# Two transformer blocks on one core: slots of the first and last round that span all four experts, tokens copied by halves

## The reference

```python
g_sel = argmax(x @ w_rg + b_rg)                        # one of 4 groups
e_sel = (x @ w_re + b_re)[group g_sel]                 # 8 logits
top_p, top_i = top_k(softmax(e_sel), 2)                # two experts
y = sum over the two: weight * (silu(x @ w_gate[e]) * (x @ w_up[e])) @ w_down[e]
```

## Time and profile before

| what | value |
|---|---|
| median of 3 runs | 1939.9 us (1939.42 to 1945.66) |
| the profiled execution | 1944.58 us, span 1942.9 us |
| mean granted PE clock | 0.918 of full |
| PE busy | 1547.8 us, 80% of the span |
| DVE, ACT, POOL busy | 424.6, 248.7, 86.5 us |
| HBM read | 708.17 MB, 365 GB/s over the span |

### The profile page before, as it was taken

The page is one execution under the profiler, slowest core; times in us unless marked ns, Lnnn a source line. Parts: engine busy times, 40 slices in busy tenths (PEclk is TensorE's granted clock), DMA queues, the critical chain, the costliest instruction groups (busy, mean ns, idle before and its releaser), DMA issues.

```text
span 1942.9 us, 23298 instructions
## 1 busy us (share of the span) xinstructions
PE 1547.8 (80%) x10236; PEld 749.9 (39%) x10236; DVE 424.6 (22%) x944; ACT 248.7 (13%) x531; POOL 86.5 (4%) x142
## 2 busy tenths in 40 slices
PE   7898777899888788999977677776798777576676
PEld 4654434764454344444522122221354222122222
DVE  3341111226331112464500000000043000000001
ACT  0310000126221011155100000000011000000000
POOL 1100000101100000112100000000000000000000
PEclk9999989999999899999998888888899888878888
DMA  7559999869869999299499999999986999999996
GB/s 283 220 217 404 423 423 423 298 225 388 314 270 410 413 421 419 94 363 399 191 403 424 423 424 423 424 424 424 423 328 269 424 424 424 424 423 424 424 423 268
DMA packets 122894, 711.11 MB, mean 366 GB/s; under 512 B 8376, under 2 KB 13480, under 8 KB 49056
## 3 DMA queue, kind: packets, MB, share of 16 engines
q1 hardware_dynamic: 116368, 697.14, 87.7%
q0 software_dynamic: 4320, 9.78, 1.4%
q10 hardware_dynamic: 2096, 2.57, 0.5%
HBM read 708.17 MB, written 1.05 MB: 365 GB/s over the span
## 4 chain that ended last, share of the span: by engine, by line
PE 46%; DMA 42%; DVE 5%; SPq 3%; ACT 2%; issue 2%; POOL 0%; DVEq 0%; ACTq 0%; PEldq 0%; POOLq 0%
DMA ring<-in_moe_w 22%; DMA ring<-in_moe_w_down 9%; PE pa L757 7%; PE pb L740 6%; DMA work<-in_moe_w 5%; PE pa L775 4%; PE acc L819 3%; PE pb L725 3%; DMA ring<-in_moe_w_up 3%; PE acc L1314 3%; PE acc L1319 3%; SPq L681 2%; PE acc L1059 2%; PE acc L1233 2%; DMA mod<-in_moe_w 2%
## 5 line engine op out<-in xcount | busy, mean ns | idle before, releaser
L740 PE MATMUL pb<-ring,XT 128*32 128x512 f32 x1488 | 274.7, 702 | 91.2 <-DMA ring<-in_moe_w 82.4
L757 PE MATMUL pa<-ring,work 128*32 128x512 f32 x1056 | 220.2, 754 | 75.7 <-DMA ring<-in_moe_w 43.9
L740 PEld LDWEIGHTS pb<-ring,XT 128*32 128x32 f32 x1488 | 64.5, 125 | 255.5 <-issue 124.7
L819 PE MATMUL acc<-XT,work 128*128 128x512 f32 x256 | 118.4, 605 | 35.2 <-DVE XT L875 22.4
L865 DVE TENSOR_TENSOR work<-work,pb 128x256 f32<-128x256 f32 (+1 forms) x32 | 17.8, 555 | 574.3 <-PE pb L740 433.7
L775 PE MATMUL pa<-work,HM 128*128 128x128 f32 x1024 | 128.4, 287 | 18.2 <-issue 18.2
L775 PEld LDWEIGHTS pa<-work,HM 128*128 128x128 f32 x1024 | 126.8, 203 | 33.0 <-issue 33.0
L740 PE MATMUL pb<-work,XT 128*32 128x512 f32 x480 | 112.0, 688 | 26.5 <-DMA work<-in_moe_w 26.5
L757 PEld LDWEIGHTS pa<-ring,work 128*32 128x32 f32 x1056 | 48.5, 132 | 200.8 <-issue 88.9
L725 PE MATMUL pb<-ring,XT 128*32 128x256 f32 x1728 | 111.7, 385 | 11.8 <-DMA ring<-in_moe_w_up 7.3
L757 PE MATMUL pa<-work 128*32 128x512 f32 x384 | 86.3, 747 | 22.0 <-DMA work<-in_moe_w 13.2
(11 more groups left out here) (404 smaller groups left out, 1741.5 us busy)
## 6 DMA issues: line engine op xcount, KB each, us to landing
ring<-in_moe_w SPq DMA_DIRECT2D x135, 2048.0 KB
work<-in_moe_w SPq DMA_DIRECT2D x46, 2048.0 KB
ring<-in_moe_w_up SPq DMA_DIRECT2D x28, 2048.0 KB
ring<-in_moe_w_gate SPq DMA_DIRECT2D x26, 2048.0 KB
ring<-in_moe_w_down SPq DMA_DIRECT2D x24, 2048.0 KB
ring<-in_w_mod SPq DMA_DIRECT2D x48, 1024.0 KB
mod<-in_moe_w SPq DMA_DIRECT2D x11, 2048.0 KB
work<-in_moe_w_down SPq DMA_DIRECT2D x8, 2048.0 KB
```

The costliest lines, as they stand in the source:

```text
L740: last = nc.tensor.matmul(hbank[m][j * CAP:(j + 1) * CAP, :], m_xg[:, k, j * CAP:(j + 1) * CAP], slot_of(s0 + j // 2)[:, at:at + fn], star ...
L757: last = nc.tensor.matmul(pa[j * CAP:(j + 1) * CAP, h, :], m_ht[:, c, j * CAP:(j + 1) * CAP], slot_of(i)[:, at:at + 512], start=(c == 0), ...
L819: last = nc.tensor.matmul(acc[:, tt, h * 512:(h + 1) * 512], m_pwt[:, tt * P:(tt + 1) * P], m_yg[:, 4 * h:4 * h + 4, :], start=False, stop ...
```

## The change

- `across` (new): in round 0 the first two slots, and in round 7 all down slots, span all four experts. A slot of the gate matrix then holds half of its rows (wide: half of the first half's) for four experts; a down slot holds one chunk of 128 hidden values for four experts. Each slot is given back by itself. In the last round the constant products stand between the chunks, 8 at a time, in place of 10 between the slots of a pair.
- The gather counts each half. ACT copies the first bank after the first half. The gate products wait for that copy alone; the wait for DVE's copies (`second_banks`) stands before chunk 4 (narrow) or before the up matrix (wide). Rounds 6 and 7 of stage 2 keep the wait in front, and so do rounds of a further pass.
- `rows_tensor` stands behind the first matrix (narrow: the gate; wide: its first half), but for those two rounds.
- Routing: 2 constant products in place of 8 before tile 1's transposes; new ones before the logits, 2 for tile 1 and, in the wide stages, 4 for tile 0.

```diff
+        def across(fn, g, i):
+            down = moe_slots(fn) - fn // P
+            if g == 0 and i < 2:
+                return 0, 0, i
+            if g == ROUNDS - 1 and i >= down:
+                return 2, (i - down) // 2, (i - down) % 2
+            return None
@@ router_tensor
-                    warm_tensor(pe, pb[:, 0, :], 8)
+                    warm_tensor(pe, pb[:, 0, :], 2)
...
+                if t or ph.fn == FN2:
+                    warm_tensor(pe, (pb[:, 0, :], pa[:, 1, :])[t], (4, 2)[t])
                 pe.wait_ge(xt_ready, 4 * ph.xt + 2 * (t + 1))
@@ whole_sync
+                slot_free(sp, q)
+                if across(ph.fn, g, i):
+                    w, half, u = across(ph.fn, g, i)
+                    src = names[w][g * SIDE:(g + 1) * SIDE].rearrange("j (h p u r) f -> h u p j (r f)", h=ph.fn // FN1, p=P, u=2)[half, u]
+                    sp.dma_start(slot(q).rearrange("p (j f) -> p j f", j=SIDE), src).then_inc(full[at[q].slot], FILL)
+                    continue
@@ new, called by whole_up_tensor for the first matrix of round 0
+        def across_up_tensor(fn, rows, s0, bank, wait_full, free, slot_of, n, at_half=None):
+            for k in range(n):
+                if at_half and k == n // 2:
+                    at_half()
+                if k % rows == 0:
+                    wait_full(s0 + k // rows)
+                held = slot_of(s0 + k // rows).rearrange("p (j r f) -> p j r f", j=SIDE, r=rows)
+                for j in range(SIDE):
+                    last = nc.tensor.matmul(bank[j * CAP:(j + 1) * CAP, :], m_xg[:, k, j * CAP:(j + 1) * CAP],
+                                            held[:, j, k % rows, :], start=(k == 0), stop=(k == KC - 1))
+                if k % rows == rows - 1:
+                    last.then_inc(*free)
@@ whole_up_tensor, narrow
+                    if across(fn, g, 2 * m):
+                        across_up_tensor(fn, KC // 2, 0, hbank[m], wait_full, free, slot_of, KC, second_banks)
+                        rows_tensor(pe, ph, g)
+                        continue
                     for k in range(KC):
+                        if m == 0 and k == KC // 2:
+                            second_banks()
...
-                    if m == 0:
+                    if m == 0 and context_round(ph, g):
                         context_tensor(pe, ph, g)
+                    elif m == 0:
+                        rows_tensor(pe, ph, g)
@@ whole_up_tensor, wide
+                    if s0 == 2:
+                        second_banks()
+                        rows_tensor(pe, ph, g)
+                    if across(fn, g, s0):
+                        across_up_tensor(fn, KC // 4, s0, hbank[m], wait_full, free, slot_of, KC // 2)
+                        continue
@@ whole_down_tensor
+            if g == ROUNDS - 1:
+                for c in range(n_down):
+                    if c:
+                        warm_tensor(pe, pb[:, 1, :], 8)
+                    wait_full(n_up + c)
+                    held = slot_of(n_up + c).rearrange("p (j f) -> p j f", j=SIDE)
+                    for h in range(2):
+                        for j in range(SIDE):
+                            last = nc.tensor.matmul(pa[j * CAP:(j + 1) * CAP, h, :], m_ht[:, c, j * CAP:(j + 1) * CAP],
+                                                    held[:, j, h * 512:(h + 1) * 512], start=(c == 0), stop=(c == n_down - 1))
+                    last.then_inc(*free)
+                return
...
-                            if g == ROUNDS - 1 and j:
-                                warm_tensor(pe, pb[:, 1, :], 10)
@@ round_tensor
-            last.then_inc(r["gathered"], 1)
+                if k % (KC // 2) == KC // 2 - 1:
+                    last.then_inc(r["gathered"], 1)
...
-            pe.wait_ge(r["pwt_copied"], t + 1 + START)
             pe.wait_ge(r["ht_copied"], t + START)
-            pe.wait_ge(r["xg_copied"], 2 * (t + 1) + START)
+            pe.wait_ge(r["xg_first"], t + 1 + START)
+            def second_banks():
+                pe.wait_ge(r["xg_copied"], t + 1 + START)
+                pe.wait_ge(r["pwt_copied"], t + 1 + START)
             if whole:
-                rows_tensor(pe, ph, g)
-                whole_up_tensor(pe, ph, g, wait_full, free, slot_of, hbank)
+                if context_round(ph, g):
+                    second_banks()
+                    rows_tensor(pe, ph, g)
+                whole_up_tensor(pe, ph, g, wait_full, free, slot_of, hbank, second_banks)
+            else:
+                second_banks()
@@ round_scalar
-            act.wait_ge(r["gathered"], t + 1 + START)
-            nc.scalar.copy(m_xg[:, 0:4, :], pa[:, 0, :].rearrange("p (k c) -> p k c", c=P)).then_inc(r["xg_copied"], 1)
+            act.wait_ge(r["gathered"], 2 * t + 1 + START)
+            nc.scalar.copy(m_xg[:, 0:4, :], pa[:, 0, :].rearrange("p (k c) -> p k c", c=P)).then_inc(r["xg_first"], 1)
```

More of the change, by code:

```diff
@@ L525, in build_model @@
         R = [{n: sem(f"{n}{k}") for n in (
-            "p_ready", "pw_ready", "rank_next", "gathered", "xg_copied", "pwt_ps", "pwt_copied", "silu_done", "hh_ready", "ht_ps", "ht_copied", "y_copied", "added")} for k in ("", "_x")]
+            "p_ready", "pw_ready", "rank_next", "gathered", "xg_first", "xg_copied", "pwt_ps", "pwt_copied", "silu_done", "hh_ready", "ht_ps", "ht_copied", "y_copied", "added")} for k in ("", "_x")]
         xfull = [sem(f"xslot{i}_full") for i in range(XSLOTS)]
@@ L677, in whole_sync @@
                     lent_wait(sp, ph, at[q].slot)
+                slot_free(sp, q)
[4 more added lines that the diff above has]
+                    continue
                 w, j, half = run_parts(ph.fn, i)[0]
                 src = names[w][g * SIDE + j:g * SIDE + j + 2].rearrange("j (h p r) f -> h p j (r f)", h=ph.fn // FN1, p=P)[half]
-                slot_free(sp, q)
                 sp.dma_start(slot(q).rearrange("p (j f) -> p j f", j=2), src).then_inc(full[at[q].slot], FILL)
@@ L713, in round_sync, with whole_up_tensor @@
                         sp.dma_start(dst[:, m * SLOT // 2:(m + 1) * SLOT // 2].rearrange("p (j f) -> p j f", j=2), src).then_inc(fills(i), inc)
-        def whole_up_tensor(pe, ph, g, wait_full, free, slot_of, hbank):
+        def across_up_tensor(fn, rows, s0, bank, wait_full, free, slot_of, n, at_half=None):
[10 more added lines that the diff above has]
+                    last.then_inc(*free)
+        def whole_up_tensor(pe, ph, g, wait_full, free, slot_of, hbank, second_banks):
             fn = ph.fn
@@ L844, in round_vector @@
             dve.wait_ge(r["rank_next"], t + START)
-            dve.wait_ge(r["gathered"], t + START)
+            dve.wait_ge(r["gathered"], 2 * t + START)
             one = m_p.rearrange("p t (j s) -> p t j s", j=SIDE)
@@ L856, in round_vector @@
             v.tensor_scalar(m_rank[:, :, ex], m_rank[:, :, ex], float(CAP), None, ALU.subtract).then_inc(r["rank_next"], 1)
-            dve.wait_ge(r["gathered"], t + 1 + START)
+            dve.wait_ge(r["gathered"], 2 * (t + 1) + START)
             v.tensor_copy(m_xg[:, 4:8, :], pa[:, 1, :].rearrange("p (k c) -> p k c", c=P)).then_inc(r["xg_copied"], 1)
@@ L1140, in rows_vector, with context_round @@
                 scaled_vector(dve, plan[ph.i + 2].ln, link, rows_before(2, 3))
+        def context_round(ph, g):
+            return ph.moe == 1 and g >= ROUNDS - TT
         def context_tensor(pe, ph, g):
-            if ph.moe == 1 and g >= ROUNDS - TT:
+            if context_round(ph, g):
                 t = g - (ROUNDS - TT)
```

## The result

| | before | after |
|---|---|---|
| runs | 7, median 1943.94 us (1939.42 to 1945.66) | 7, median 1924.93 us (1921.99 to 1932.87) |
| the profiled execution | 1944.58 us | 1922.37 us, span 1920.6 us |
| mean granted PE clock | 0.918 | 0.921 |

The ratio is 0.9913, 95% interval [0.99, 0.9925]: faster by 0.9%, 17 to 19 us, where the forecast was 22.9 from 1939.9 to 1917.0. The runs of after lie in two groups, 1922 to 1925 (five) and 1931 to 1933 (two); unchanged, it gave 1926.52 in a second set (1924.87 to 1932.18). The four later sets of before gave medians of 1943.5 (11 runs), 1942.4 (19), 1945.7 (11) and 1944.2 (15): the 1939.9 that I started from was a low draw of three, and medians of different sets are comparable to about 3 us only.

A forecast was written before the change was run, and what follows sets the result against it. DMA was taken to bound the expert stages, except at their starts and ends. Starts 3.7, 4.7, 4.8, 5.9, dip 1.0, two ends of 1.8, less 0.8 for packets: 22.9 us, from 1939.9 to 1917.0; range 1911 to 1927.

The forecast's parts named there:

- The starts: Fronts of the four expert stages: transfers restart earlier, by 3.7, 4.7, 4.8 and 5.9 us.
- Stage 1: Start of the first expert stage: routing 0.9, copy by halves 1.0, across slots 1.8, together 3.7 us.
- second release: Stage 2, round 1's gate slots given back: 4.9 us earlier, 4.7 after a loss of 0.2 at the up slots.
- Stage 3: Start of the third expert stage: routing 2.0, copy by halves 1.0, across slots 1.75, together 4.8 us.
- the routing: Fewer constant products before tile 1's transposes: 0.9, 0.9, 2.0 and 1.1 us in stages 1 to 4.
- Stage 4: Start of the fourth expert stage: routing 1.1, copy 1.0, rows 2.0, across slots 1.75, together 5.9 us.
- the dip: Stage 2 at 668 to 676, ended by round 4's gate release: 1.0 us gained, 0 to 1.0.
- the shorter ends of stages 2 and 4: Behind the last slot, 16 instructions in place of 28: 1.8 us gained in each of the two stages.
- packets: Across slots read 4 KB runs in place of 8 KB: 0.1 us a slot, 0.8 us lost in all.
- A: Rival: fewer routing products let PE's clock fall, about 4.5 us a start; 1926 for two, 1935 for four; chance 0.16.
- B: Rival: reading four experts at once halves the rate, 4.96 us more per across slot on the path; 1957; chance 0.03.
- C: Rival: the first slot alone does not restart the queue, so the across terms go; 1922; chance 0.07.

The follow-up runs named there:

- calm: changed kernel plus constant products in waits: 10 for 6 before ranks, 10 behind stage 3's last scatter, 6 and 8 in sparse attention; 1920.52 us, ratio 0.9877.

## Why the forecast was right in its first part and wrong in its second

**The starts: the mechanism right, the sum to 0.1 us by luck (19.18 for 3.7 + 4.7 + 4.8 + 5.9 = 19.1).** Stage 1 is 1.15 short and stage 3 1.20 over, both mainly by PE's clock; the two errors cancel.
Stage 1 gave 2.55 for 3.7: 1.6 went to the half clock in the gather; where it holds (`calm`) it is 4.18, of which about 0.6 is the fall that before has in this start (25.36 for 24.76 in the one of its versions without it).
Stage 2, second release: 4.95 for 4.9.
Stage 3: 6.00 for 4.8. The mis-sized term is the routing, 2.0 taken, 2.7 to 3.3 measured, and most of it is clock: five of six traces with the old routing fall to half clock ahead of tile 1 in this stage. The sixth (halves and rows) holds it there; its A3 to R3 of 28.57 is 2.81 over the filled kernel's, which leaves 1.1 for the routing after the 1.75 of the across slots (an estimate). The 4 constants that I priced at nothing stand in the 1.13 us wait before tile 0's logits, and in the twelve traces that have them the clock never falls at this place.
Stage 4: 5.68 for 5.9.
Across and rows have their prices in the runs that undo them: 1.74 and 1.71 for 1.8 and 1.75; 4.2 for 4.

**What failed: the sum past the starts.** The step is the one where I added the dip and the shorter ends of stages 2 and 4 in full to what the starts give: 1.0 for the dip, 1.8 each for the two ends, less 0.8 for packets, together 3.8. Measured: +0.53 (R1 to W), -0.45 (R2 to C), -1.38 and +1.37 (end of stage 3 and the Fourier mixer), +1.47 - 1.68 (stage 4), in sum a gain of 0.1. In the filled kernel it is 0.8.

*Stage 2* ("What counts is that second release"; 4.7 + 1.0 + 1.8 = 7.5). The last scatter came 5.40 earlier, counted from A2 (234.56 to 229.16). The dip gave its 0.9. But the transfers missing in the 12 us behind the release (by windows of 1 us, each (423 - rate)/423) rose from 1.37 to 2.31 us. I had 0.2 for it, and that was already wrong by its own numbers: 5.5 against 6.5 less 1.6 is 0.6. The other part is that the first refills of the stage are issued 5.5 earlier (26.68 to 21.18 behind A2) and are through sooner, so that the transfers run dry 0.4 us before the second release (0.3 behind it in before); then the one gate refill lasts 4.96 while the up slots' come 5.50 later (3.45 before). Round 6's second down slot, the last that PE waits for, is 4.48 earlier. From there PE sets the pace to the end, and what stands in it gained 0.92 for the 1.8: 1.69 from the last slot's products to the scatter (2.73 for 4.42), less 0.49 (28 products 5.81 for 5.32, more of them at half clock) and less 0.28 for the rows, which start 1.55 behind the transposes for 1.27 (PE waits 1.16 there for DVE's copy, 0.90 before). Moving rows frees a slot earlier and makes PE's round no shorter, as I wrote; I had not asked how long the stage's end is PE's. Nor do the parts of this stage add: from before (A2 to C 238.10) halves and rows give 1.4 (236.67) for the 5.0 that I had for them and the dip, the new routing 1.0 more (235.67), and the across slots 3.0 (232.70). These are single traces, and the clock moves A2 to C by up to 2 us between executions of one kernel (234.43 in the second trace of after).

*Stage 4* ("slot at 1925.1. 1.8"). The queue of PE was as forecast (free before the slot, which it waited 1.01 for), and L to O is 1.68 shorter. But the slot came 1.47 later after the restart. Windows of after and of the second trace of before, over the last six and five us ahead of the last products (1904.57 and 1922.20):

```profile
1899.00:1901.00 2.00, 1.35 (x16) 0.42 (x16) 0.00 (x0) 0.00 (x0) 0.00 (x0) 1.00 0.69 283
1901.00:1903.00 2.00, 2.00 (x21) 1.49 (x14) 0.00 (x0) 0.00 (x0) 0.00 (x0) 1.00 0.40 166
1903.00:1905.00 2.00, 0.99 (x10) 0.52 (x12) 0.00 (x0) 0.00 (x0) 0.00 (x0) 1.00 0.04 16
```

```profile
1917.00:1919.00 2.00, 1.98 (x11) 0.78 (x10) 0.00 (x0) 0.00 (x0) 0.00 (x0) 1.00 0.86 365
1919.00:1921.00 2.00, 1.86 (x17) 1.67 (x15) 0.00 (x0) 0.00 (x0) 0.00 (x0) 1.00 0.53 225
1921.00:1923.00 2.00, 0.80 (x8) 0.29 (x12) 0.00 (x0) 0.00 (x0) 0.00 (x0) 1.00 0.06 25
```

The rate leaves 420 GB/s 431 to 432.5 us after the restart in every kernel. Then the share of the engines falls step by step (0.69, 0.40, 0.04 in after), as if the 16 finished one after another, and the slot counts when the last is through: after about 4.0 us in the four traces of before and its filled versions, 4.5 to 6.0 in the twelve of the changed kernel, filled or with a part undone (read to 0.5 us). R4 to L needs no such reading: 435.54 to 435.74 in the four, 436.19 to 437.88 in the twelve. In after the last two microseconds have a share of 0.04, less than one engine of 16. No part is the cause by itself: without the 4 KB packets of the last slots the drain is 5.5, without any across slots 5.0, without the new routing 6.0, and halves with rows alone give 4.0, the routing alone 4.5. What parts the engines stays open.

*Stage 3.* Its 0 held, but as the difference of two things that I had not forecast: 1.38 won at the end, 1.37 lost at the Fourier mixer's start, where the clock fell behind a wait of 2.80 us. Before has the same wait and kept the clock in both traces, but lost it with only the sparse attention filled, so the fall is not the change's doing alone. But it is far more frequent with it: in 10 of the 11 traces that hold the halves or the rows and no fill behind the last scatter, in 1 of the 4 that hold neither, in 0 of the 3 with that fill. Why is open. The timeline of PE in that kernel:

```profile
1418.52 3.40 PE L1643 MATMUL pa<-early,HM 128*128 128x256 f32 x8 [2.80 <-DVE HM L482]
```

*Packets.* 0.1 us a slot was about right. A window of after in the last round:

```profile
1887.00:1890.00 3.00, 2.14 (x18) 0.60 (x11) 0.69 (x1) 0.00 (x0) 0.00 (x0) 1.00 1.03 411
```

411 for 422 is 0.13 us a slot. The Trainium skill, "DMA: Bandwidth & Descriptors", section "Why small descriptors are slow", gives, by the prediction's estimate from its bus overhead, 0.06 a slot; the measurement is about twice that, and decides.

**The rivals.** A (the clock falls in the routing) happened, but not for the reason given. With the new routing and no fills 14 of 40 gathers were slow, 0.5 to 1.6 us each; with the old routing 0 of 24, with the new routing and fills 0 of 8. That is not the count of falls, though. The granted clock shows half clock between A and R in 12 of the 24 starts with the old routing too, only earlier, ahead of the ranks (the 3.66 us group above), where DVE's chain hides a part. So taking products out did not make the clock fall more often; it moved the fall into the gather, where nothing hides it. A fall there costs about 1.6 us at a restart (22.81 for 21.18 in stage 1), where I had 4.5; one more fall in the old routing cost 0.6 (A3 to R3 31.77 for 31.16). The fills on before could not help, as its falls stand ahead of the wait that was filled. By the Trainium skill, "TensorE: Matmul & The Clock Gate", section on the HAM clock gate, activity is what lifts the clock. The 0 of 8 with the wait filled agrees; that taking products out must speak against the change does not follow, as the 14 of 40 against 12 of 24 show. B and C are out: four experts are read at 411, and the first slot restarts the queue.

**The medians** differ by 17 to 19 us, the change's own segments in the two profiled executions by 19.3. With its waits filled the changed kernel is 23.5 under the kernel before with the same fills, so the forecast's size was there to be had, by another way than the forecast's: against the first trace of before, the filled kernel's starts give 20.8 and the rest of the change 0.8.

## What to carry to other kernels

Sum the starts and the ends apart: a restart that comes earlier is worth its full microseconds only up to the next place where PE or an empty queue sets the pace, and a shorter tail behind the last slot is worth what the slot's arrival leaves of it. Where constants are taken out of a chain, look for the wait that becomes longer, here the one before the ranks (0.82 to 1.29 us), and put them there: A to R is no longer for it in any stage. Together with the fills in the sparse attention and behind the last scatter it took the median from 1925.6 (13 runs) to 1920.5, and the spread from 11 us to 0.8 (4 runs); the fill before the ranks was not run by itself. And count the falls of the clock in both kernels before putting them down to the change. Prove a part by the segment that it touches, across several traces, when the clock moves the total by more than the part is worth.

## What the runs showed of the hardware that was not expected

- The same instructions in an untouched stretch took 133.4 to 138.9 us in executions of one kernel, as PE's clock fell or not behind waits of 2.0 and 2.4 us.
- With a queue full of 2 MB transfers running dry, the last one lands about 4 to 6 us after the rate leaves 420 GB/s, and this differs between kernels that read the same bytes in the same order of stages.
- The half clock fell in 12 of 24 starts with the old routing and in 14 of 40 with the new one; it reached the gather in none of the 24 and in all of the 14.
- By the medians, undoing one part cost 7 to 10 us in each of four cases (33 in sum) where the whole is worth 17 to 19; by the ratios to before it is 3 to 9 (28 in sum), the least for the routing. Their traces also differ in where the clock falls. Undoing the last-round slots cost nothing.
